# A one-core layer step on Trainium2: weight sums moved ahead of finishing work, operands of group B prepared earlier, another timetable for attention, other output banks

## The reference, cut to what matters

```python
h = rmsnorm(x, g_pre);  z = h @ w_in            # 61 column tiles of 128
q, k, v, ga, qi, ki, wi, bg, cg, hc, gb = split(z)
# attention group
iscore = sum_h relu(qi_h @ ki.T) * wi_h         # 16 index heads of 64
sel    = top_k(iscore, 256)                     # chunk-causal; 132 for samples
attn   = softmax(q @ k[sel].T) @ v[sel]         # 8 heads, 2 key heads
# convolution group
conv   = bg * conv3(cg * hc)                    # causal, width 3
y      = x + rmsnorm(concat(attn * silu(ga), conv * silu(gb)) @ w_out, g_post)
```

## Time and profile before

| | |
|---|---|
| median of 3 runs | 2425.06 us |
| profiled execution, its own time | 2424.28 us |
| its span, first to last instruction | 2422.4 us |
| PE busy | 2169.0 us (90%) |
| DVE busy | 1427.8 us (59%) |
| POOL busy | 1046.3 us (43%) |
| ACT busy | 829.5 us (34%) |
| granted clock of PE, mean | 0.959 |
| DMA queue of SP | 281.14 MB, 35.6% of 16 engines |

### The profile page before, as it was taken

How to read it: one execution, slowest core, us unless ns; L and a number is a source line. 1 busy time by engine, 2 the same in 40 slices (tenths; PEclk the granted TensorE clock), 3 DMA queues, 4 the chain that set the end, 5 groups by cost and what they waited for, 6 DMA issues and landing times.

```text
span 2422.4 us, 29498 instructions
## 1 busy us (share of the span) xinstructions
PE 2169.0 (90%) x11309; PEld 1893.2 (78%) x11309; DVE 1427.8 (59%) x2122; ACT 829.5 (34%) x1195; POOL 1046.3 (43%) x414
## 2 busy tenths in 40 slices
PE   4799999999999968898899798899897899989996
PEld 4799998999999966776677687687676778868885
DVE  7775555555555587886721598999886334352102
ACT  6433333233333434334323432232233333342221
POOL 4577777666666842332221133333222232333331
PEclk9899999999999989999999999999999999999998
DMA  5443322222222245434354422222322443266433
GB/s 203 140 146 103 121 91 76 84 76 94 83 76 81 101 161 143 112 115 138 123 153 155 117 83 86 86 83 101 109 79 70 135 135 115 92 200 220 144 122 122
DMA packets 167356, 283.04 MB, mean 117 GB/s; under 512 B 43312, under 2 KB 97584, under 8 KB 166448
## 3 DMA queue, kind: packets, MB, share of 16 engines
q1 hardware_dynamic: 167216, 281.14, 35.6%
HBM read 239.53 MB, written 41.56 MB: 116 GB/s over the span
## 4 chain that ended last, share of the span: by engine, by line
PE 64%; DVE 24%; issue 4%; ACT 3%; POOL 2%; DMA 2%; SPq 0%; DVEq 0%; ACTq 0%
PE ps L1106 22%; PE ps L1173 17%; PE ps L1206 17%; DVE isc L2000 4%; PE ps L1227 4%; DVE top L1999 4%; POOL w_lo L1059 2%; PE ps L1274 2%; DVE isc L1986 1%; PE ps L1079 1%; DVE ev L1851 1%; DVE ev L1838 1%; DVE w_sum L1725 1%; ACT w_hi L1369 1%; PE ps L1337 1%
## 5 line engine op out<-in xcount | busy, mean ns | idle before, releaser
L1059 POOL TENSOR_TENSOR w_lo<-w_raw,w_hi 128x1024 fp32r<-128x1024 f32 x338 | 871.9, 2585 | 1171.1 <-ACT w_hi L1369 1171.1
L1106 PE MATMUL ps<-xop,w_hi 128*128 128x320 f32 x3424 | 774.8, 315 | 88.1 <-POOL w_lo L1059 80.6
L1106 PEld LDWEIGHTS ps<-xop,w_hi 128*128 128x128 f32 x3424 | 588.0, 193 | 94.0 <-DVE ev L1824 45.9
L1369 ACT ACTIVATE w_hi<-w_raw 128x1024 fp32r<-128x1024 f32 x338 | 357.7, 1059 | 624.0 <-PE ps L1106 226.9
L1106 PE MATMUL ps<-xop,w_lo 128*128 128x320 f32 x1712 | 537.6, 314 | 0.0
L1173 PE MATMUL ps<-act_hi,w_hi 128*128 128x512 f32 x976 | 399.1, 409 | 20.5 <-DVE ev L1824 17.1
L1173 PE MATMUL ps<-act_lo,w_hi 128*128 128x512 f32 x976 | 392.7, 402 | 0.0
L1173 PE MATMUL ps<-act_hi,w_lo 128*128 128x512 f32 x976 | 391.2, 401 | 0.0
L1106 PEld LDWEIGHTS ps<-xop,w_lo 128*128 128x128 f32 x1712 | 330.4, 193 | 0.0
L1824 DVE TENSOR_TENSOR ev<-ev,ps 128x320 f32<-128x320 f32 x240 | 109.0, 485 | 318.2 <-PE ps L1106 274.9
L1059 POOL TENSOR_TENSOR w_lo<-w_sum,w_hi 128x1024 fp32r<-128x1024 f32 x61 | 173.1, 2838 | 166.1 <-ACT w_hi L1369 166.1
(11 more groups left out here) (193 smaller groups left out, 2340.3 us busy)
## 6 DMA issues: line engine op xcount, KB each, us to landing
w_raw<-in_w_in SPq DMA_DIRECT2D x244, 512.0 KB, 4.4
w_raw<-in_w_out SPq DMA_DIRECT2D x64, 512.0 KB, 4.5
conv<-in_x_prompt SPq DMA_DIRECT2D x16, 512.0 KB, 5.3
conv<-z_mix SPq DMA_DIRECT2D x32, 256.0 KB, 3.6
qraw<-z_qi SPq DMA_DIRECT2D x24, 256.0 KB, 4.5
x<-in_x_a SPq DMA_DIRECT2D x8, 640.0 KB, 10.4
out<-o_nat SPq DMA_DIRECT2D x10, 512.0 KB, 3.1
qraw<-z_q SPq DMA_DIRECT2D x16, 256.0 KB, 3.0
```

Of the source, the lines that this page charges most:

```text
L1059: nc.gpsimd.tensor_tensor(w_lo[:, r], weight_source(h), w_hi[:, r].bitcast(F32), ALU.subtract).then_inc(sem_w_lo, 1)
L1106: last = nc.tensor.matmul(ps[:, bank, 0:HALF_A], wt[:, o % RING, k], xop[:, u, part, k], start=(start and k == 0 and wt is w_hi and part = ...
L1369: return nc.scalar.activation(out, in_, ACT.Copy)
```

## The change

1. **Start.** DVE scales x11 and x22 in place (`scaled`) and ACT only copies the hi parts; ACT scales x21 and x12 once, in place (`scale_block`). All operand sums become plain adds of 640 columns. Squares move later. The roots of A and their spread move from pair 0 to pair 1, and `finish(0)` to product 1 of pair 1.
2. **Pairs.** At product 0 DVE has `combine(p-1, 7)`, then the sums for product 3, then `finish(p-1)`. The taps of cg tiles move behind the sums for product 4.
3. **x of B.** Ten places (`XB`). Ten loads go out in pair 26, their scalings stand in pairs 27 and 28, the other six in the last pair at product 3. `act_hi` and `act_lo` become two halves of `act_parts`, so that piece k overlays operand k//5 of the last pair. `combine(29, 7)` comes after all lo parts, the gate of pair 29 after the first weight copy of B, and the attention starts six slots later.
4. **Timetable.** New sections: TK of "s" beside the softmax of A for key head 0, TK.4 beside the softmax of the streams, TK.5 beside that of A for key head 1, more slots for `rounds7` and `last`. The keys of the indexer of B are loaded twice.
5. **Output.** z of A comes through six places, its hi and lo parts two slots later than before. The first four products of B go to banks 4 to 7 and wait for the last attention results, no longer for the squares of A's last output tiles.

```diff
@@ def z_pieces / z_loads
-    n, s = divmod(slot, SLOTS)
+    n, s = divmod(slot - 2, SLOTS)
...
-        return [(0, k) for k in range(KT) if s == max(0, (k - 4) // 2)]
+        return [(0, k) for k in range(KT) if s == min(max(0, (k - 2) // 2), 7)]
@@ SECTIONS, timetable
-SECTIONS = dict(heads2=10, rounds2=33, rounds3=48, softmax_a=65, streams=34, heads4=10, rounds4=48, rounds5=57, rounds6=64,
-                rounds7=76, last=16)
+SECTIONS = dict(heads2=10, rounds2=34, rounds3=48, rounds_s=38, heads4=10, rounds4=40, rounds5=66, rounds6=58, rounds7=100,
+                last=30)
...
-    at = section(at, size["softmax_a"], softmax_steps("A", US_B), rounds("s"))
-    at = section(at, size["streams"], stream_softmax_steps())
-    at = section(at, size["heads4"], [(("IK", "B"), W["keys"])] + heads(4))
-    for b in (4, 5, 6):
-        at = section(at, size[f"rounds{b}"], rounds(b), heads(b + 1))
+    at = section(at, size["rounds_s"], rounds("s"), softmax_a[:half_a])
+    at = section(at, size["heads4"], [(("IK", "B", 4), W["keys"])] + heads(4))
+    at = section(at, size["rounds4"], rounds(4), stream_softmax_steps() + heads(5))
+    at = section(at, size["rounds5"], rounds(5), [(step, 2) for step in second_a] + softmax_a[half_a:]
+                 + [(("IK", "B", 6), W["keys"])] + heads(6))
+    at = section(at, size["rounds6"], rounds(6), heads(7))
     at = section(at, size["rounds7"], rounds(7), softmax_b[:cut])
@@ z_place, xb_slot, act
-            r = k % 4
+            r = k % (4 if g else 6)
...
-        act_hi = sb("act_hi", [P, KT, T_B], F32R)
-        act_lo = sb("act_lo", [P, KT, T_B], F32R)
+        act_parts = sb("act_parts", [P, KT, 2, T_B], F32R)
+        act_hi, act_lo = act_parts[:, :, 0], act_parts[:, :, 1]
@@ out_place, PE's waits
-            return ps[:, use % 4 if pair < PAIRS else (use - 4 * PAIRS) % 8, 0:OW]
+            return ps[:, use % 4 if pair < PAIRS else (use - 4 * PAIRS + 4) % 8, 0:OW]
...
+                        elif use < 4 * PAIRS + 4:
+                            pe.wait_ge(sem_z_dve, UNITS)
                         else:
-                            pe.wait_ge(sem_nat_sq, max(use - 7, 4 * PAIRS))
-                            if use == 4 * PAIRS + 4:
-                                pe.wait_ge(sem_z_dve, UNITS)
+                            pe.wait_ge(sem_nat_sq, use - 7)
@@ ACT
-                act.wait_ge(sem_gemm, OPS_A - PAIR_OPS + (3 if k < 14 else 4))
-                copy(act_hi[:, k], xb_slot[k % 7]).then_inc(sem_xb_hi, 1)
+                act.wait_ge(sem_gemm, OPS_A - PAIR_OPS + k // 5 + 1)
+                copy(act_hi[:, k], xb_slot[k % XB]).then_inc(sem_xb_hi, 1)
@@ DVE, start
-                for k in range(CHUNK * c, CHUNK * (c + 1)):
-                    last = nc.vector.scalar_tensor_tensor(out=out[:, k], in0=src[:, k], scalar=g_t[:, k + 8 * j:k + 8 * j + 1],
-                                                          in1=other[:, k], op0=ALU.mult, op1=op)
-                last.then_inc(sem_x_sum, 1)
+                nc.vector.tensor_tensor(out[:, k], one[:, k], other[:, k], op).then_inc(sem_x_sum, 1)
...
+            def scaled(name, c):
...
+                for k in range(CHUNK * c, CHUNK * (c + 1)):
+                    last = nc.vector.tensor_scalar(block_of[:, k], block_of[:, k], g_t[:, k + 8 * at:k + 8 * at + 1], None,
+                                                   ALU.mult)
+                last.then_inc(sem_x_sc, 1)
@@ DVE, loop over pairs
                     if p and i == 0:
-                        finish(p - 1)
+                        combine(p - 1, 7)
+                        sums_ahead(FIRST_OPS + PAIR_OPS * p + 3)
+                        if p == 1:
+                            root_diagonals("A")
+                        else:
+                            dve.wait_ge(sem_cmb, 8 * p)
+                            finish(p - 1)
...
+                    if p and i == 1 and TILES[pair_tiles(p - 1)[0]][1] == "cg":
+                        taps("A", TILES[pair_tiles(p - 1)[0]][2])
...
-                    if p == NPAIR - 1 and i == 1:
-                        for k in range(4):
+                    if p in (NPAIR - 3, NPAIR - 2) and 1 <= i <= 5:
+                        xb_scale(5 * (p - NPAIR + 3) + i - 1)
+                    if p == NPAIR - 1 and i == 3:
+                        for k in range(10, KT):
                             xb_scale(k)
-                    if p == NPAIR - 1 and i >= 3:
-                        for k in range(4 * (i - 3), 4 * (i - 2)):
-                            if k + 4 < KT:
-                                xb_scale(k + 4)
+                    if p == NPAIR - 1 and i in (1, 2, 4):
+                        for k in {1: range(5), 2: range(5, 10), 4: range(10, KT)}[i]:
                             xb_low(k)
+            combine(NPAIR - 1, 7)
```

274 lines of the change are left out of this document (145 added, 129 removed).

## The result

The changed kernel took 2394.57 us in the median of four runs (2391.70 to 2396.04), the kernel before 2423.03 (2418.07 to 2426.05): a ratio of 0.9883, interval 0.9862 to 0.9904. It is faster by 28.5 us where 101 were forecast, and lies outside the range. The profiled spans are 2422.4 and 2389.9 us; the profiled execution of the changed kernel is the fastest of its four, so the traces differ by 32.5 us.

What follows compares the result with a forecast made beforehand. PE was taken as the bound everywhere, with its idle time and lower clock to win. Terms -40 - 15 - 22 - 6 - 8 - 10 = -101 us took 2424.28 to 2323 us; range 2272 to 2370.

Steps and rivals of the forecast that it cites:

- Ready between 11.5 and 14.8 us: Pairs: POOL's lo part for product 4, due at 14.0 us; 1.2 us left per pair, for a term of -40 us.
- 0.9 us at the sum: Pairs: DVE and POOL delay each other at the sum itself by up to 0.9 us (3.31 against 2.41).
- at nothing: Pairs 27 and 28: scalings moved out of the last pair cost nothing beside products with 7 us of slack; uncovered, 7.
- Start: -15: Start, change 1: 5.2 + 7 + 3 us of PE's waits go, from -8 to -22.
- The 12.03: Start: PE's longest wait, at 77.44 us, was to fall from 12.03 to 5 us.
- nothing net: Start: one bound for the fall in DVE's work, which was anything from 10 us to nothing net.
- the spread's 5.2: Start: PE's 5.16 us wait for the roots' spread goes, since it moves behind a product of pair 1.
- A to B: Group A to B, change 3: shorter waits for DVE and the first HEAD, 11 + 7 + 4, -22 us (-8 to -30).
- the outputs: Output, change 5: shorter waits at the start of A's and B's outputs, -8 and -10 us; bounds together -8 to -21.
- Attention: -6: Attention, change 4: idle 92.3 us becomes 73 to 92, less 8 lost in rounds6; -6 us, bounds -40 and +35.
- 8 to 10%: Attention: PE's idle share over the whole, making the 92.3 us of idle time 73 to 92.
- the pairs' wait only moves: Rival, chance 0.19: pairs' wait moves to product 4, start stays DVE-bound; -40 becomes -10, -15 becomes -5; 2363 us.

Runs made afterwards that it cites:

- its twin: Old order on DVE in the pairs, with POOL's lo parts made for the first eighth only, from pair 10 to the end of A; 2335.58 us, 0.9645.

## Why the prediction was wrong

By the traces the forecast missed by 68 us: 26 in the pairs, 21 in the attention, 13.5 at the start and 10 in pairs 27 to 29; the other terms brought 2.5 more than forecast.

**Pairs: the step that failed.** "Ready between 11.5 and 14.8 us", with 1.2 us left per pair, was built by taking DVE's durations alone and adding one stall of 2.4 us, for product 4 behind a cg pair only. There it came to its upper end: PE starts product 4 at 418.78, 14.9 us after the pair's first matmul. Two things lay outside it. Behind a bg pair, which I didn't work out, product 4 starts after 16.7 us (447.55): the sum for product 3 and the first sum for product 4 stall for 2 us each (L1743, L1745), and product 4 needs two sums (L1745, L1747) where I counted one. And behind a cg pair the stalled taps (L1893) stand ahead of the sum for product 6, whose wait the forecast doesn't have. Of the waits over 0.3 us in pairs 11 to 26, product 4 has 24.3 us in 16 (19 forecast), product 6 has 9.1 in 8, product 3 has 1.6 in 2. In place of 19 us, 36.6 are left of 41.8. What was won is mostly the lower clock: 91 matmuls fewer at 0.267 us instead of 0.147, some 11 of the 13.7 us.

I named the meeting of the two engines and charged it 0.9 us at the sum; the Trainium skill ("SBUF — State Buffer", section "SBUF: two separate sides") says that the one that starts first holds the shared ports for its whole instruction, and the trace agrees in the rows above. The mistake was to apply it to the one instruction that was moved, and not to all the work that POOL's new start falls on. In the kernel before, POOL waited for the late sum, and this kept it out of DVE's way for 7.09 us.

That POOL's long instruction is the cause is shown by the run with the short one, and that no order is at fault by itself by its twin. That run doesn't divide what goes by DVE's stalls from what is POOL's own time. By the figures given with it, behind the bg pair DVE's delay is the larger part (5.25 us against 1.9), and either alone would make up for nearly all of the wait of 1.98. How the loss divides over DVE's work stays open: taking POOL work away alone won 3 us in the trace of the pairs, adding DVE work cost half of it.

**Pairs 27 to 29: "at nothing" was +10.2.** The price if uncovered was put at 7. By the timeline the moved scalings cost 4.2 of it: pair 27 has no wait over 0.3 us, but its scalings, stalled beside POOL, push DVE's sum for product 1 of the next pair back, and with it POOL's instruction for which the sum for product 3 waits, so that pairs 28 and 29 wait 2.10 and 2.12 us at product 3. The 4.25 us before the last product are another thing: there the sum for product 6 stands behind ten lo parts of x of B on DVE (from 852.10 to 864.7), which change 3 puts ahead of it and for which my sum had no term. The run with that sum first shows it, and that the lo parts then delay B instead. It is the loss beside POOL again, since the run with the short POOL instruction doesn't have it (61.3 us ahead at pair 27, 62.5 at the end of group A), and the run with the old order has it.

**Start: -15 was -1.5.** The 12.03 fell to 9.29, not to 5. The sums that became plain adds went from 23.6 to 16.5 us and DVE's scalings took 7.1, so its work stayed the same, the end of my bounds called "nothing net". Pair 1 began 14.1 us earlier, 7.7 of it because the spread with its wait now stands inside it; but I let the spread's 5.2 go because its sources had 3.5 us more, without asking what DVE has to do before the roots: with the pair 14 us earlier, the wait became 8.34. Of that, 2.5 is the sum placed ahead of the roots (shown). In the run that shows it two operations on the way to the roots, 128x5 elements each (L1720, L1721), took 2.10 and 2.26 us beside POOL and 0.16 in the changed kernel, so stalls stay there too; the rest wasn't taken apart.

**A to B and the outputs: right.** -22.4 for -22 (12.7 up to B's first matmul, 9.7 behind it) and -20.1 for -18; of the outputs 13 are shown by their own run. For the whole kernel only the 12.7 count: with the early beginning the stretch behind B's first matmul gains 0.7 instead of 9.7, and the time is the same.

**Attention: -6 was +14.9**, inside its bounds. Two things are in it. The 12 us that the later beginning covers up to the 192nd matmul are lost again behind it (954.3 us with the early beginning, 972.3 with the late, both with the old table): there PE waits 14 us longer for `pt_lo`, a part that DVE makes for the softmax. And the new table costs 9 to 12 us by the medians, though the profiled execution with the old one is only 2.8 us shorter in this stretch; that one is the slowest of its four, and that of the changed kernel the fastest. Its idle time is that of before (96.0 and 96.7 us of the two windows), while PE is busy 15.6 us longer with as many matmuls within some ten (3891 and 3883 records), at 0.95 for 0.96. So the share of idle time came out at 9.8%, the upper edge of what I forecast (8 to 10%) and hardly below the 10.1% of before; and what I left out is the lower clock: the same idle time brought more of it. The traces show how. 17 waits are over 2.5 us where 12 were, the clock fell 20 times instead of 13, and PE executed for 78.4 us at the lower clock instead of 53.2. In the three traces with the old table that I counted the clock fell 12 to 14 times, in the other one with the new table 19 times. Of PE's waits those for the scores and for the softmax on DVE grew (after twice, then before; the second one of before is in the earlier trace rows, L2048):

```profile
PE ps L1240 <- DVE isc L2005: 10.0, 6, 2.7
PE ps L1092 <- DVE F L2067: 30.2, 9, 7.2
PE ps L1227 <- DVE isc L1986: 1.1, 2, 0.9
```

Which of the moved steps does it wasn't tried.

Of the rivals "the pairs' wait only moves", with the start bound by DVE, comes closest: it gave -10 and -5 for those two terms and 2363, and its ground, that POOL and DVE take turns from the start of the pair, is what the runs show. It too lacked pairs 27 to 29 and the attention.

## What to carry to other kernels

When a wait is removed by starting an engine earlier, list everything that then runs beside it, and take the durations under that engine from rows where the two already met, not from rows where one stood still: an idle engine before the change may be what keeps its neighbour fast. If two engines stall each other, reordering can cut a wait into pieces that cost less (14 us here), but it leaves most of the idle time; here only less work of the longer instruction took it away, and giving some of it to the other engine paid only together with an earlier sum. Time won ahead of a stretch counts only if that stretch then ends earlier too: compare the start of the same matmul at each boundary, and see where it is given back.

## What was not expected of the hardware

Small instructions with a single input stall as well: the COPY of 128x16 at L1863 took 2.24 us beside POOL, one of the same size 3 us later, at L1867, 0.17. A stall also adds up over the whole of POOL's back-to-back run: four taps took 8.37 us beside 8.06 us of POOL. And of the waits of up to 2.1 us in pairs 11 to 26 only two brought the lower clock, so that cutting 16 waits into 32 gave it back though the idle time hardly fell, while in the attention the same idle time, with more waits of over 2.5 us, cost more of it.
